# Twenty-four tokens instead of sixteen through gathered expert rows in an encoder block with product-key experts

## The reference

```python
def peer_ffn(x, w_query, sub_keys, expert_u, expert_v):
    ...
        q = (xb @ w_query).reshape(TB, PH, 2, PEER_QUERY_DIM // 2)
        s = jnp.einsum('thpd,hpkd->thpk', q, sub_keys).astype(jnp.float32)
        v_half, i_half = lax.top_k(s, K)
        ...
        top_s, pos = lax.top_k(cand.reshape(TB, PH, K * K), K)
        idx = jnp.take_along_axis(cidx.reshape(TB, PH, K * K), pos, axis=-1)
        g = jax.nn.softmax(top_s, axis=-1).astype(xb.dtype)
        u = expert_u[idx]
        a = jax.nn.gelu(jnp.einsum('td,thkd->thk', xb, u), approximate=False)
        return jnp.einsum('thk,thkd->td', g * a, expert_v[idx])
```

## Time and profile before

| | |
|---|---|
| median of 3 runs | 944.01 us (942.79 to 944.62) |
| the profiled execution, its own time | 944.44 us |
| its span, first to last instruction | 942.6 us |
| granted clock of TensorE, mean | 0.999 |
| share of the span busy: PE, DVE, ACT, POOL | 99%, 83%, 62%, 36% |
| moved by DMA | 246.55 MB, mean 262 GB/s |
| an expert tile, from issue to landing | 4.6 us (3.3 to 8.2) |

### The profile page before, as it was taken

How to read it: one execution, slowest core, us unless ns; L and a number is a source line. 1 busy time by engine, 2 the same in 40 slices (tenths; PEclk the granted TensorE clock), 3 DMA queues, 4 the chain that set the end, 5 groups by cost and what they waited for, 6 DMA issues and landing times.

```text
span 942.6 us, 20282 instructions
## 1 busy us (share of the span) xinstructions
PE 934.7 (99%) x6660; PEld 881.9 (94%) x6660; DVE 783.7 (83%) x1578; ACT 580.4 (62%) x1078; POOL 343.6 (36%) x202
## 2 busy tenths in 40 slices
PE   9999999999999999999999999999999999999997
PEld 9999899999999999999999999999999999999997
DVE  7988877888799988888888987877788888888766
ACT  6555764656655547888788876655555555555545
POOL 0000000056878686888888877101100000010000
PEclk9999999999999999999999999999999999999999
DMA  8877668665688898999999998999999999999881
GB/s 300 267 235 217 202 199 237 199 218 194 186 252 234 242 255 193 254 284 285 229 257 291 236 258 248 320 346 319 319 313 319 344 330 319 319 326 313 290 267 46
DMA packets 133432, 246.55 MB, mean 262 GB/s; under 512 B 31136, under 2 KB 80160, under 8 KB 133104
## 3 DMA queue, kind: packets, MB, share of 16 engines
q1 hardware_dynamic: 110656, 227.73, 74.9%
q0 software_dynamic: 22272, 17.12, 9.5%
q10 hardware_dynamic: 432, 0.80, 0.3%
HBM read 219.21 MB, written 26.35 MB: 260 GB/s over the span
## 4 chain that ended last, share of the span: by engine, by line
PE 94%; DVE 3%; issue 1%; ACT 1%; DMA 1%; DVEq 0%; ACTq 0%
PE pOO L1507 29%; PE pMM L1515 8%; PE pOO L1515 8%; PE pTT L1819 6%; PE pMM L1819 6%; PE pOO L1819 6%; PE pSS L1819 6%; PE pOO L1516 4%; PE pMM L1516 4%; PE pOO L1820 3%; PE pMM L1820 3%; PE pTT L1820 3%; PE pSS L1820 3%; DVE wlos L958 1%; PE pSS L1581 1%
## 5 line engine op out<-in xcount | busy, mean ns | idle before, releaser
L679 ACT ACTIVATE whis<-raw 128x1024 fp32r<-128x1024 f32 x326 | 343.8, 1057 | 171.5 <-PE pSS L1820 145.1
L654 POOL DMA_INDIRECT g_scratch<-small x120 | 219.4, 1828 | 49.7 <-issue 35.1
L958 DVE TENSOR_TENSOR wlos<-raw,whis 128x1024 fp32r<-128x1024 f32 x172 | 208.9, 1218 | 20.0 <-ACT whis L679 19.1
L1386 DVE TENSOR_TENSOR wlos<-raw,whis 128x1024 fp32r<-128x1024 f32 x125 | 153.0, 1224 | 66.9 <-ACT whis L679 66.9
L1507 PE MATMUL pOO<-xpair,whis 128*128 128x240 f32 (+1 forms) x1184 | 205.6, 278 | 0.0
L1507 PEld LDWEIGHTS pOO<-xpair,whis 128*128 128x128 f32 x1184 | 179.0, 189 | 1.4 <-issue 1.4
L1507 PE MATMUL pOO<-xpair,wlos 128*128 128x240 f32 (+1 forms) x592 | 163.4, 276 | 0.0
L619 POOL TENSOR_TENSOR wlos<-raw,whis 128x1024 fp32r<-128x1024 f32 x30 | 72.2, 2414 | 214.4 <-ACT whis L679 214.3
L1515 PE MATMUL pMM<-xpair,whis 128*128 128x480 f32 x336 | 112.4, 379 | 0.0
L1507 PEld LDWEIGHTS pOO<-xpair,wlos 128*128 128x128 f32 x592 | 111.6, 188 | 0.0
L1515 PE MATMUL pOO<-xpair,whis 128*128 128x480 f32 x336 | 111.4, 379 | 0.0
(11 more groups left out here) (300 smaller groups left out, 2066.0 us busy)
## 6 DMA issues: line engine op xcount, KB each, us to landing
raw<-in_stream SPq DMA_DIRECT2D x199, 512.0 KB, 4.6
raw<-in_vrows SPq DMA_DIRECT2D x128, 512.0 KB, 4.7
a_scratch<-ast SPq DMA_DIRECT2D x128, 120.0 KB
held<-a_scratch SPq DMA_DIRECT2D x128, 120.0 KB, 4.8
g_scratch<-ghot SPq DMA_DIRECT2D x32, 256.0 KB, 4.3
G<-g_scratch SPq DMA_DIRECT2D x124, 64.0 KB, 4.5
biasm<-in_bias SPq DMA_DIRECT2D x8, 256.0 KB, 5.7
g_scratch<-small POOLq DMA_INDIRECT x128
```

What stands on the lines that cost most here:

```text
L654: pool.indirect_dma_start(g_dram, bass.IndirectOffsetOnAxis(goff[:, n:n + 1], 0), gval[:, h, k:k + 1], None, compute_op=ALU.add).then_inc( ...
L679: act.activation(whi[s], raw[s][:], ACT.Copy).then_inc(hi_ready, 1)
L958: dve.tensor_tensor(wlo[t % RING], raw[t % RING][:], whi[t % RING].bitcast(F32), ALU.subtract).then_inc(lo_ready, 1)
L1386: dve.tensor_tensor(wlo[s], raw[s][:], whi[s].bitcast(F32), ALU.subtract).then_inc(lo_ready, 1)
```

## The change

24 tokens are done apart in place of 16, so `NU` is 232 and G takes 26 steps. The 128 picks of a token no longer lie head by head on 8 partitions: they are cut in 5 shares of 26 (the last has 24 and two zeros), so 5 x 24 = 120 partitions with 26 picks each. So there are 26 gathers of u and 26 of v, of 120 rows, in place of 16 and 16 of 128 rows. 6 dots are done in U, at the tiles of `DOT_TILES_U`, and 20 in V. In V the string `V_OPS` gives the order of the 46 operations, one every 12/5 tiles from tile 10 on, the last after tile 118; POOL issues each gather 9 tiles ahead of its operation. DVE's loop over groups is written out tile by tile. gelu and shares come in three parts (6, 10 and 10 picks). In a slot of `vpair`, `ghi` begins 256 numbers (1024 bytes) behind `glo` in place of right behind it. `held` grows by 8 rows, and G shrinks by as much.

```diff
 GTOK = 4
 GSUB = 2
-G_STEPS = (P - 16) // GTOK
+APART = 24
+G_STEPS = (P - APART) // GTOK
...
-APART = 16
 NU = T - APART
-DOTS_U = 8
-DOT_TILES_U = (76, 84, 92, 100, 113, 117, 121, 124)
-GATHERS_U = {3: (0, 1), 4: (2, 3), 5: (4,), 6: (5, 6), 7: (7,)}
+SHARES = 5
+PARTS = SHARES * APART
+PICKS = 26
+DOTS_U = 6
+DOT_TILES_U = (76, 84, 92, 100, 110, 117)
+GATHERS_U = {3: (0, 1), 4: (2, 3), 5: (4,), 6: (5,)}
+ENDS = (0, 6, 16, 26)
...
-DOT_TILES = (3, 7, 16, 20, 28, 32, 41, 45)
-DOT_GROUPS = (2, 3, 6, 7, 9, 10, 12, 13)
-GELU_GROUPS = (2, 15)
-SHARE_GROUPS = (3, 16)
-ROW_TILES = (11, 24, 37, 49, 53, 58, 62, 66, 70, 74, 79, 83, 87, 91, 95, 100)
-ROW_GROUPS = (4, 8, 11, 14, 15, 16, 17, 18, 19, 20, 21, 22, 23, 24, 25, 27)
+V_OPS = "ddrddrddrddrddrr" + "dddrdrdrdrdrdrdrdrrr" + "r" * 10
+OP_FIRST, GATHER_LEAD = 10, 9
+GELU_GROUPS = (2, 12, 23)
...
+def op_tile(n):
+
+    return OP_FIRST + n * 12 // 5
+
+
+DOT_AT = {op_tile(n): DOTS_U + V_OPS[:n].count("d") for n in range(len(V_OPS)) if V_OPS[n] == "d"}
+ROW_AT = {op_tile(n): V_OPS[:n].count("r") for n in range(len(V_OPS)) if V_OPS[n] == "r"}
+SHARES_AT = tuple(min(t for t in ROW_AT if ROW_AT[t] == m) for m in ENDS[:-1])
...
-        held = sbs(top, "held", [P, 113, NK])
+        held = sbs(top, "held", [P, 121, NK])
...
-        gpair = [vpair[:, s, 0:2 * NU].rearrange("p (q n) -> p q n", q=2) for s in range(RING)]
+        gpair = [vpair[:, s].rearrange("p (q n) -> p q n", q=2)[:, :, 0:NU] for s in range(RING)]
         glo = [vpair[:, s, 0:NU] for s in range(RING)]
-        ghi = [vpair[:, s, NU:2 * NU] for s in range(RING)]
+        ghi = [vpair[:, s, V_SLOT // 2:V_SLOT // 2 + NU] for s in range(RING)]
...
-            for i in range(ROW_TILES[-1] + 1):
-                if i in DOT_TILES:
-                    pool.wait_ge(tile_done, T_V + i)
-                    gather_u(DOTS_U + DOT_TILES.index(i))
-                if i in ROW_TILES:
-                    pool.wait_ge(tile_done, T_V + i)
-                    gather_v(ROW_TILES.index(i))
+            for n in range(len(V_OPS)):
+                at = op_tile(n)
+                pool.wait_ge(tile_done, T_V + at - GATHER_LEAD)
+                if at in DOT_AT:
+                    gather_u(DOT_AT[at])
+                else:
+                    gather_v(ROW_AT[at])
...
+            dve.memset(picks, 0.0)
...
-            def groups(first, end):
-
-                with dve.Fori(first, end) as g:
-                    for s in range(4):
-                        next_parts(g * 4 + s, s, g + ((s + 2) // 4 + 1))
...
+            for i in range(RING, NE_TILES - 4):
+                next_parts(i, i % 4, (i + 2) // 4 + 1)
+                if i in SHARES_AT:
+                    gates_apart(SHARES_AT.index(i))
+                if i in DOT_AT:
+                    dot(DOT_AT[i])
+                if i in ROW_AT:
+                    add_row(ROW_AT[i])
...
-            pe.wait_ge(rows_added, TOPK)
+            pe.wait_ge(rows_added, PICKS)
```

More of the change, by code:

```diff
@@ L289, in build @@
         wfull = [piece(8 + 2 * s, 2)[:, 0:NU] for s in range(2)]
-        urow = [piece(12 + 8 * s, 8) for s in range(U_BUFS + V_BUFS)]
-        xall = piece(76, 8)
-        yacc = piece(84, 8)
-        gpair = [vpair[:, s, 0:2 * NU].rearrange("p (q n) -> p q n", q=2) for s in range(RING)]
+        urow = [piece(12 + 8 * s, 8)[0:PARTS] for s in range(U_BUFS + V_BUFS)]
+        xall = piece(76, 8)[0:PARTS]
+        yacc = piece(84, 8)[0:PARTS]
+        gpair = [vpair[:, s].rearrange("p (q n) -> p q n", q=2)[:, :, 0:NU] for s in range(RING)]
         glo = [vpair[:, s, 0:NU] for s in range(RING)]
-        ghi = [vpair[:, s, NU:2 * NU] for s in range(RING)]
[L296 to L300, removed]
+        ghi = [vpair[:, s, V_SLOT // 2:V_SLOT // 2 + NU] for s in range(RING)]
+        uoff = small[0:PARTS, 2, 0:PICKS].bitcast(U32)
+        dots = small[0:PARTS, 2, PICKS:2 * PICKS]
+        shares = small[0:PARTS, 2, 2 * PICKS:3 * PICKS]
+        picks = small[0:PARTS, 5, 0:3 * PICKS].rearrange("p (a k) -> p a k", a=3)
+        chosen = small[0:PARTS, 3, 0:APART]
         ident2 = small[:, 4, :]
@@ L528, in stored, with load_picks, load_xrows @@
                 sp.wait_ge(a_stored[i % AST], 16 * (i // AST + 1))
[L531 to L533 removed]
+            def load_picks(g):
+                if g == 0:
                     sp.wait_ge(routed, 1)
[L535 to L539 removed]
+                n = min(PICKS, PH * TOPK - g * PICKS)
+                mine = route[P - APART:P, 1].rearrange("p a h k -> p a (h k)")[:, :, g * PICKS:g * PICKS + n]
+                sp.dma_start(picks[g * APART:(g + 1) * APART, :, 0:n], mine).then_inc(picks_landed, 16)
+            def load_xrows(g):
+                if g == 0:
                     sp.wait_ge(xtok_stored, 16)
                     sp.wait_ge(gbanks_free, 2)
[L542 removed]
+                sp.dma_start(xall[g * APART:(g + 1) * APART], x_dram).then_inc(x_landed_apart, 16)
             for t in range(T_U, T_V):
@@ L901, in gelu_dots @@
             def gelu_dots(part):
-                act.wait_ge(dots_done, TOPK if part else DOTS_U)
-                at = slice(DOTS_U, TOPK) if part else slice(0, DOTS_U)
+                act.wait_ge(dots_done, ENDS[part + 1])
+                at = slice(ENDS[part], ENDS[part + 1])
                 act.activation(dots[:, at], dots[:, at], ACT.Gelu).then_inc(dots_gelu, 1)
[L907 to L911, removed]
+            first = 1
+            for part, end in enumerate(GELU_GROUPS):
+                groups(first, end)
+                gelu_dots(part)
+                first = end
+            groups(first, NE_TILES // 4 - 1)
             for i in range(NE_TILES - 4, NE_TILES - 2):
@@ L1242, in _ @@
             dve.tensor_copy(ident2, ident)
-            dve.tensor_reduce(chosen, ident.rearrange("p (h t) -> p t h", t=APART), AX_X, ALU.add)
+            dve.tensor_reduce(chosen, ident[0:PARTS, 0:PARTS].rearrange("p (g t) -> p t g", t=APART), AX_X, ALU.add)
+            dve.memset(picks, 0.0)
             dve.tensor_copy(steps16, K("iota16"))
@@ L1362, in add_row @@
                 row = urow[U_BUFS + m % V_BUFS]
-                dve.wait_ge(shares_ready, 1 if m < DOTS_U else 2)
+                dve.wait_ge(shares_ready, sum(m >= e for e in ENDS[:-1]))
                 dve.wait_ge(urow_landed[U_BUFS + m % V_BUFS], 16 * (m // V_BUFS + 1))
```

8 lines of the change are left out of this document (4 added, 4 removed).

## The result

The changed kernel takes 996.81 us (median of 4 runs, 992.66 to 997.57) where the kernel before takes 943.40 (4 runs, 942.57 to 944.62): a ratio of 1.0556, 95% interval 1.0532 to 1.0581. It is 5.6% slower, 62 us above the forecast and far outside its range. The forecast's step on DMA fell, and it costs more than all the others bring.

The account below looks back on a forecast made before the run. TensorE (PE), busy 934.7 of 942.6 us, was taken as the bound. Columns 11.3 plus G steps 1.0 minus seam stall 3.0 gave 9.3 us off 944.44: 935.1, or 934.7 as median; range 929.5 to 944.5.

Parts of the forecast that it names:

- step 1: U and V stages: wide pairs with 464 instead of 480 columns save 6.7 ns each on PE, 11.3 us.
- the floor: Narrow U matmuls: the next weight's load, about 112 ns, is the longer, so 232 columns cost what 240 cost.
- the rival by columns: Each matmul is paid by its columns, 8 fewer saving 3.3 ns; only V gains, 931.3 us; chance 0.14.
- step 2: U stage: 26 G steps instead of 28 save 1.0 us of PE.
- step 3: V stage: the operand split into two runs 1024 bytes apart costs nothing, at most 0.5 us.
- step 4: V stage: 22 more DVE operations, 26 us of work, fit in DVE's idle time and cost nothing.
- step 5: V stage: 46 POOL gathers, each asked for 9 tiles ahead of its use, cost nothing.
- step 6: V stage: DMA traffic rises to 357 GB/s from 331, which the engines can give; cost nothing.
- The slower rival: V tiles 10 to 118: DMA engines give only 331 GB/s, adding 21.5 us, 956.2; chance 0.09 together with DVE.
- step 7: Seam from U to V: PE stalls 3.0 us for G's first loads; bounds nothing and 5.5 us.
- term of 0.4 for POOL's lighter chain: Seam from U to V: two gathers fewer in POOL's chain were taken to shorten PE's stall by 0.4 us.

Follow-up runs that it names:

- variant with the earlier start: Changed kernel with 128-row gathers and the gap; POOL makes 16 U low parts instead of 17, DVE takes one over, so POOL's scatters can start earlier: 933.36 us.

## Why the prediction was wrong, point by point

- **Columns (step 1): right.** A wide U pair went from 327 to 319.3 ns, a V pair from 326.5 to 321.6 with the gap and 320.0 without. The narrow U trios stayed at 335 ns, 111.7 a matmul with 232 columns as with 240, so the floor holds (that the weight load sets it is the prediction's reading of the earlier trace rows, and no run varied the load), and the rival by columns (325) falls.
- **G steps (step 2): not shown.** U ends 7.6 us earlier with 128 rows (590.02 against 597.66), 6.9 in the kernel after, 5.1 in the one without the gap, where steps 1 and 2 made it 5.5 and the wide pairs alone bring 672 x 7.7 ns = 5.2. So the end of U varies by 2.5 us among kernels whose U is the same; what lies in the 1.0 of the G steps can't be read from it.
- **The gap (step 3): nearly right.** It brings nothing, as forecast, but by the pitch it costs 1.6 us where the upper end was 0.5; the intervals of the two times overlap. V gained 5.1 us with 128 rows (339.8 us from its first matmul to the end, against 344.8) and not 6.8, and by the pitch that is this term.
- **DVE (step 4): right.** With 128 rows DVE is 87 to 90% busy in V, and PE doesn't wait. The waits on DVE in the kernel after are inherited from the DMA.
- **Gathers (step 5): landings later than reckoned, at no cost.** A gather of v landed in 8.6 to 11.8 us, median 10.1 (5.8 to 7.8 before), well inside its 9 tiles, and DVE shows no wait for one. The gathers harmed nobody by being late; they harmed by keeping the DMA engines (step 6).
- **DMA (step 6): this step failed.** It priced a gather by its bytes, 120 x 4 KB, as if 120 rows were 120/128 of the gather in the trace. They are 31.2 us of engine time against 24.4 in the kernel before: 28% more, not 6% less. The error is in the treatment of an operation that the trace of before doesn't show: a gather of 120 rows was taken for the gather of 128 in the trace and given no bound of its own. Priced by the kernel before with 120 rows, the stretch of 2.4 tiles and a gather needs 1.70 MB x 49.0 + 31.2 = 114.5 us of engine, by 16 engines at a share of 1.05 6.82 us, where PE asks for it every 6.14: 45 x 0.68 = 30 us too much, about half of the 62 us by which V was missed. With the two prices of the kernel after, 53.3 and 32.5, it is 7.33 us, 45 x 1.19 = 53. But that second figure explains nothing of its own: where the engines are full, their time per MB is the measured slowness written another way. What it says is where the rest went, into slower transfers of the other queue, and that could be seen only in the changed kernel. 2.3 us more are the slow clock of V's first tile; the remainder isn't split up.
- **The slower rival** had the right place (V tiles 10 to 118), mechanism (the DMA engines as the bound) and signature (ACT waiting for experts). Its price was too low, 21.5 us against some 55 (V against V before), as its ceiling of 331 GB/s was a rate of bytes, while the bound was the engines' time, which the shape of the gathers sets. It got a chance of 0.09 together with DVE, and against it stood 400 GB/s over five microseconds and the few waits of the earlier trace rows; neither touches step 6's unspoken assumption.
- **The seam (step 7): right in kind, not steady.** 4.8 us of idle PE in the kernel after, 4.6 in one of the variants, none in four others; where it came, the slow clock behind it added 2.3 and 2.8 us, for which the step had no term. The forecast of 3.0 lies between, but its term of 0.4 for POOL's lighter chain has no meaning where that chain's end moves by 10 us between kernels that differ little.

With 128 rows the change is worth about what was forecast: 933.53 us against 934.7, ratio 0.9897. That the two lie so close is in part luck. In the profiled executions U gained 7.6 us where 5.5 were forecast, the seam took nothing where 3.0 were, and V gained 5.1 where 6.8 were; these errors partly cancel. Together with its variant with the earlier start (933.36) it is the fastest complete kernel of the study, 1.0% under the kernel before and 6.3% under the changed one.

## What to carry to other kernels

When a change alters the shape of a transfer, take its price as unknown and bound it, even if its bytes hardly move; the list of queues gives engine time per row, which is the unit to reckon with, and GB/s doesn't. A row was cheapest here in a gather to all 128 partitions, also where some of them fetch rows that nobody reads, and the changed kernel was 63 us faster with 128 rows than with 120, and 28 us faster than with 112 or 96: where a count is near 128, try padding the indices. That a much smaller gather should be padded isn't shown: in the kernel before, one of 64 rows took 15.6 us of an engine and one of 128 rows 24.4. And where two variants differ by a few microseconds, look first whether a seam elsewhere has moved before crediting the edit, and count the slow clock behind it with its idle time.

## What the runs showed of the hardware that was not expected

- A gathered row of 4 KB costs 0.176 to 0.191 us of an engine in gathers of 128 rows, and 0.234 to 0.270 in gathers of 64, 96, 112 and 120, with 120 the dearest; and these gathers slow the plain transfers beside them, from 45.1 to 53.3 us of an engine per MB in the same kernel.
- One core moved 368 GB/s over 200 us (with 128 rows), at a DMA share of 1.02; the same share went with 289 GB/s from 800 to 900 us of the kernel with 120 rows. The share tells that the engines are full, not how much they move.
- The granted clock fell where PE had waited. At the seam of the kernel after it stood at 1.00 while PE was busy, at 0.50 from 594 to 600 us, behind PE's 4.8 us of idle time, and at 1.00 again from 602 us on, with PE busy since 595.85. Within the slowed V stage, 840 to 850 us, where PE was busy for 7.41 of 10 us, shows 0.83, a mean of the two levels.

```profile
840.00:850.00 10.00, 7.41 (x34) 6.54 (x35) 7.88 (x13) 4.41 (x7) 1.26 (x1) 0.83 0.89 259
850.00:860.00 10.00, 10.00 (x65) 9.30 (x64) 7.85 (x15) 5.04 (x8) 1.17 (x1) 1.00 1.04 284
```

So a wait can make the matmuls after it slower too: 2.3 us at the seam. What it cost within V isn't shown (0.98 in the last of the three windows, 1.00 in the others), since there PE waited for the DMA engines anyway.
